# Attention of two blocks: groups in pairs on TensorE, the sink's column as the start of the minimum, scaling on GpSimd

## The reference

```
m = jnp.max(s, axis=-1)
m = jnp.maximum(m, sk)                      # sk: the sink of the head
p = jnp.exp(s - m[..., None])
l = jnp.sum(p, axis=-1) + jnp.exp(sk - m)
p = p / l[..., None]
o = jnp.einsum('bnhgqk,bnkhd->bnqhgd', p, vv)
```

## Time and profile before

| | us |
|---|---|
| median of 3 runs (lowest, highest) | 2098.12 (2096.47, 2103.21) |
| the profiled execution | 2096.36 |
| its span | 2094.6 |
| stage a, scores of group 2 to last sums | 1063.85 to 1127.80 |
| stage b, first scores to last sums | 1610.18 to 1686.30 |

### The profile page before, as it was taken

One profiled execution on the slowest core, in us unless ns is written; L12 is line 12 of the kernel. 1 busy time (PEld: TensorE's weight loads), 2 busy tenths in 40 slices (PEclk: granted clock), 3 DMA queues, 4 the chain that ended last, 5 costly groups with the idle time before them and its releaser, 6 DMA issues.

```text
span 2094.6 us, 28597 instructions
## 1 busy us (share of the span) xinstructions
PE 2059.3 (98%) x10618; PEld 1733.8 (83%) x10618; DVE 986.8 (47%) x1909; ACT 886.8 (42%) x1307; POOL 844.6 (40%) x281
## 2 busy tenths in 40 slices
PE   9999999999999999998999999999999999999998
PEld 6888877888888888884878888888887688888887
DVE  4889688573411111366985344134323934431432
ACT  3355445363443222534366454233423954432332
POOL 3443432444244444442712444444443034444443
PEclk9999999999999999999999999999999999999999
DMA  9654312325233342341202432433422034324322
GB/s 370 243 184 125 101 61 61 94 93 181 72 104 86 104 116 78 111 117 43 79 13 57 120 100 86 115 101 95 145 86 73 2 96 119 101 79 122 100 73 88
DMA packets 303799, 219.63 MB, mean 105 GB/s; under 512 B 13568, under 2 KB 288128, under 8 KB 301408
## 3 DMA queue, kind: packets, MB, share of 16 engines
q1 hardware_dynamic: 293216, 195.67, 31.1%
q10 hardware_dynamic: 10496, 22.81, 3.5%
HBM read 213.48 MB, written 2.10 MB: 103 GB/s over the span
## 4 chain that ended last, share of the span: by engine, by line
PE 64%; issue 18%; DVE 10%; POOL 5%; ACT 3%; ACTq 0%; POOLq 0%; DMA 0%; DVEq 0%
PE bank L900 51%; POOL w_split L2783 5%; PE bank L1123 2%; PE bank L1313 2%; PE bank L1335 2%; DVE bank L2280 2%; DVE arena L2743 1%; DVE small L2741 1%; DVE bank L2243 1%; PE bank L1322 1%; PE bank L1171 1%; DVE bank L2222 1%; POOL w_split_out L2783 1%; PE bank L1418 1%; PE bank L1271 1%
## 5 line engine op out<-in xcount | busy, mean ns | idle before, releaser
L900 PE MATMUL bank<-h_hi,w_split 128*128 128x512 f32 x3696 | 1119.3, 381 | 0.7 <-POOL w_split L2783 0.7
L2783 POOL TENSOR_TENSOR w_split<-wslots,w_split 128x2048 fp32r<-128x2048 f32 (+3 forms) x174 | 712.7, 4096 | 971.1 <-ACT w_split L1581 530.5
L900 PEld LDWEIGHTS bank<-h_hi,w_split 128*128 128x128 f32 x3696 | 698.0, 189 | 116.6 <-issue 17.5
L900 PE MATMUL bank<-h_lo,w_split 128*128 128x512 f32 x1848 | 701.3, 379 | 0.0
L900 PEld LDWEIGHTS bank<-h_lo,w_split 128*128 128x128 f32 x1848 | 349.3, 189 | 52.7 <-issue 5.2
L900 PE MATMUL bank<-hid_hi,w_split 128*128 128x512 f32 x1056 | 315.8, 379 | 1.9 <-DVE hid_lo L2525 1.9
L1602 ACT ACTIVATE w_split<-wslots 128x2048 fp32r<-128x2048 f32 (+2 forms) x80 | 141.3, 1767 | 367.9 <-PE bank L900 367.9
L1581 ACT ACTIVATE w_split<-wslots 128x2048 fp32r<-128x2048 f32 (+3 forms) x91 | 158.7, 1744 | 312.8 <-PE bank L900 287.1
L900 PEld LDWEIGHTS bank<-hid_hi,w_split 128*128 128x128 f32 x1056 | 199.6, 189 | 31.5 <-DVE hid_lo L2525 3.2
L900 PE MATMUL bank<-hid_lo,w_split 128*128 128x512 f32 x528 | 200.1, 379 | 0.0
L2243 DVE SCALAR_TENSOR_TENSOR bank<-arena,cols,bank 128x512 f32<-128x512 f32 x240 | 161.4, 749 | 5.5 <-ACT bank L1695 4.9
(11 more groups left out here) (342 smaller groups left out, 2353.3 us busy)
## 6 DMA issues: line engine op xcount, KB each, us to landing
wslots<-in_f_w_up SPq DMA_DIRECT2D x88, 512.0 KB, 4.8
wslots<-in_w_in SPq DMA_DIRECT2D x24, 1024.0 KB, 5.4
wslots<-in_w_ffn_up SPq DMA_DIRECT2D x44, 512.0 KB, 4.6
arena<-in_w_ada ACTq DMA_DIRECT2D x8, 2048.0 KB, 8.9
wslots<-in_f_w_down SPq DMA_DIRECT2D x16, 768.0 KB, 4.8
wslots<-in_a_w_in SPq DMA_DIRECT2D x10, 1024.0 KB, 5.2
wslots<-in_f_w_down SPq DMA_DIRECT2D x16, 640.0 KB, 4.5
arena<-in_w_ada_first SPq DMA_DIRECT2D x8, 1024.0 KB, 18.9
```

Of the source, the lines that this page charges most:

```text
L900: return nc.tensor.matmul(bank[:], w, woven(x), start=start, stop=stop)
L2783: last = nc.gpsimd.tensor_tensor(part[:, 1, cols_of], slot(p, 1, size)[:, 0, cols_of], part[:, 0, cols_of].bitcast(F32), ALU.subtract)
```

## The change

TensorE takes the groups in pairs: step i is scores(2i), scores(2i+1), turn(2i-3), turn(2i-2), sums(2i-5), sums(2i-4). On DVE the minimum of a group with a sink begins from the sink's column, so `lowest` goes; the reciprocal hands over to GpSimd, which scales the probabilities; the copies of odd groups go to DVE, those of even groups stay on ACT, each with a semaphore of its own. GpSimd's first four pieces of the output weights follow the groups 30 to 33, the second four the last group. The memory queries' pieces move to before the first turns. Two semaphores of memsets become one.

```diff
@@ TensorE, attend
-                for g in range(len(groups) + SUM_LAG):
-                    if g < len(groups):
-                        scores(g)
-                    if g in FILL_AT:
-                        next(fill)
-                    if g in early:
-                        early[g]()
-                    if LAG <= g < len(groups) + LAG:
-                        turn(g - LAG)
-                    if g >= SUM_LAG:
-                        sums(g - SUM_LAG)
+                steps = len(groups) // 2
+                for i in range(steps + 3):
+                    of_groups = lambda part, first: [part(g) for g in (first, first + 1) if 0 <= g < len(groups)]
+                    of_groups(scores, 2 * i)
+                    if i in (steps, steps + 1):
+                        next(fill)
+                    if ("turn", i) in early:
+                        early["turn", i]()
+                    of_groups(turn, 2 * i - 3)
+                    if i in (steps, steps + 1):
+                        next(fill)
+                    if ("sums", i) in early:
+                        early["sums", i]()
+                    of_groups(sums, 2 * i - 5)
...
+            def queries_end():
+                mem_queries(2 * DT - 3)
+                mem_queries(2 * DT - 2)
+
+            attend(2, b_fill, {("turn", 0): queries_end, ("turn", 1): lambda: mem_queries(2 * DT - 1),
+                               ("sums", 2): lambda: wait_emptied(pe, "b_qmem")})
@@ ScalarE, attend
-                    if with_sink:
-                        act.wait_ge(S["at_lowest"], g + 1)
-                    else:
-                        act.wait_ge(S["at_logits"], n + 1)
+                    act.wait_ge(S["at_logits"], n + 1)
...
-                for g in range(len(groups) + SUM_LAG):
+                for g in range(len(groups) + 6):
                     if g < len(groups):
                         exps(g)
-                    if LAG <= g < len(groups) + LAG:
-                        copies(g - LAG)
-                    if g >= SUM_LAG and (g - SUM_LAG) % TB == TB - 1:
-                        outputs(g - SUM_LAG)
-                    if g - len(ATTENTION[k]) in SPLIT_AT:
...
+                    if g % 2 == 0 and 2 <= g < len(groups) + 2:
+                        copies(g - 2)
+                    if g % TB == 0 and g >= 2 * TB:
+                        outputs(g - 5)
+                    if g in SPLIT_AT:
...
@@ VectorE, attend
-                        ins = nc.vector.tensor_tensor_reduce(out=out, in0=src, in1=mask, scale=-grp["scale"], scalar=-NEG, op0=op, op1=ALU.min,
+                        least = -NEG if sink is None else cols[:, COL["sinks"] + sink + e:COL["sinks"] + sink + e + 1]
+                        ins = nc.vector.tensor_tensor_reduce(out=out, in0=src, in1=mask, scale=-grp["scale"], scalar=least, op0=op, op1=ALU.min,
...
-                    steps.did(nc.vector.reciprocal(stat(n, 0, ne), stat(n, 4, ne)))
+                    nc.vector.reciprocal(stat(n, 0, ne), stat(n, 4, ne)).then_inc(S["at_inverse"], 1)
...
+                def copies(g):
...
+                    dve.wait_ge(S["at_turned"], n + 1)
+                    if n >= 3:
+                        dve.wait_ge(S["at_sums"], n - 2)
+                    w = groups[g]["n"]
+                    nc.vector.tensor_copy(probs_turned[:, n % 3, 0:w], banks[6 + n % 2][:, 0:w]).then_inc(S["odd_copied"], 1)
...
+                for g in range(len(groups) + 8):
                     if g < len(groups):
                         logits(g)
                     if 1 <= g <= len(groups):
                         inverses(g - 1)
...
+                    if g == 3 and early:
                         early()
...
+                    if g % 2 and 5 <= g < len(groups) + 4:
+                        copies(g - 4)
+                    if g % TB == 2 and g >= 10:
+                        lower(g - 7)
@@ GpSimd
+            def attend(k, output):
+
+                g0, groups = GROUPS_BEFORE[k], ATTENTION[k] + ATTENTION[k + 1]
+                for g, grp in enumerate(groups):
+                    n = g0 + g
+                    pool.wait_ge(S["at_inverse"], n + 1)
+                    for e, (lo, w) in enumerate(grp["heads"]):
+                        part = probs[:, n % RING, lo:lo + w]
+                        last = nc.gpsimd.tensor_scalar(part, part, stat(n, e), None, ALU.mult)
+                    last.then_inc(S["at_probs"], 1)
+                    if 30 <= g < 34:
+                        lower_piece(output, ahead(output), g - 30)
+                for piece in range(4):
+                    lower_piece(output, 1 - ahead(output), piece)
```

More of the change, by code:

```diff
@@ L2011, in copies @@
                     w = groups[g]["n"]
[L2012 removed]
+                    nc.scalar.activation(probs_turned[:, n % 3, 0:w], banks[6 + n % 2][:, 0:w], ACT.Copy).then_inc(S["even_copied"], 1)
                 def outputs(g):
@@ L2627, in inverses @@
                     dve.wait_ge(S["at_exp"], n + 1)
-                    steps.did(nc.vector.reciprocal(stat(n, 0, ne), stat(n, 4, ne)))
-                def weights(g):
+                    nc.vector.reciprocal(stat(n, 0, ne), stat(n, 4, ne)).then_inc(S["at_inverse"], 1)
+                def copies(g):
                     n = g0 + g
-                    steps.settle()
-                    for e, (lo, w) in enumerate(groups[g]["heads"]):
-                        part = probs[:, n % RING, lo:lo + w]
-                        last = nc.vector.tensor_scalar(part, part, stat(n, e), None, ALU.mult)
-                    last.then_inc(S["at_probs"], 1)
+                    dve.wait_ge(S["at_turned"], n + 1)
[3 more added lines that the diff above has]
+                    nc.vector.tensor_copy(probs_turned[:, n % 3, 0:w], banks[6 + n % 2][:, 0:w]).then_inc(S["odd_copied"], 1)
                 def lower(g):
@@ L2643, in lower @@
                     nc.vector.tensor_tensor(out, unit_bank(n // TB)[:], upper.bitcast(F32), ALU.subtract).then_inc(S["at_low"], 1)
-                for g in range(len(groups) + SUM_LAG + 1):
+                for g in range(len(groups) + 8):
                     if g < len(groups):
@@ L2650, in attend @@
                         inverses(g - 1)
-                    if g < len(groups):
-                        lowest(g)
-                    if 1 <= g <= len(groups):
-                        weights(g - 1)
-                    if g == LAG and early:
+                    if g == 3 and early:
                         early()
-                    if g > SUM_LAG and (g - SUM_LAG) % TB == 0:
-                        lower(g - SUM_LAG - 1)
+                    if g % 2 and 5 <= g < len(groups) + 4:
+                        copies(g - 4)
+                    if g % TB == 2 and g >= 10:
+                        lower(g - 7)
             def ffn(k):
```

55 lines of the change are left out of this document (26 added, 29 removed).

## The result

The changed kernel takes 2117.82 us, median of 4 runs (2115.89 to 2119.52), beside 2099.55 for the kernel before (2096.47 to 2103.21): ratio 1.0077 [1.0064, 1.0090]. It is slower by 0.8%, where 2088 us (2080 to 2098) was forecast. The profiled execution has a span of 2114.3 us against 2094.6.

What follows compares the result with a forecast made beforehand. TensorE, 98% busy, was taken as the bound, with DVE and ACT close. Window gains 1.5 + 0.4 + 1.7 + 2.3 + 0.9 + 2.6 = 9.4 us from 2096.36 gave 2087.0, set to 2088 with half the median's surplus; range 2080 to 2098.

Steps and rivals of the forecast that it cites:

- The step that failed: GpSimd's scaling of 256 columns in both attention stages: 0.40 us, 0.80 a group, with 0.70 as the other end.
- The forecast's loop: Steady stage b: in-order queues tie ACT, DVE and TensorE in a loop over four groups, 6.28 us, above the 5.58 floor.
- the port: Steady stage b: DVE's sink copy waits while GpSimd scales, some 0.2 us, making the loop 6.5 a turn.
- Rival B: Both stages: GpSimd scales at 0.70 us and the loop goes through it, 7.0 a turn; 2094 to 2096 us; chance 0.19.
- Rival D: Both stages, worst in b: scaling over 0.83 us makes GpSimd the bound; about 2112 us at 1.05; chance 0.10.
- Rival C: Both stages: the loop has slack and TensorE runs at its floors; 2081 us; chance 0.14.
- Rival E: TensorE: gaps come with handing over, not tile shape, so pairs keep them; only starts and tails gain, 2093 us; chance 0.05.
- A head: Steady stage a: a head falls from 5.50 to 5.43 us, gaining 0.4 us in that window.
- The pairs: TensorE: changes of tile shape, 0.53 us a group, are paid once for two groups; four b groups' floor 5.58.
- worth nothing alone: ACT: losing half its copies, 0.24 us a group, gains nothing alone because ACT is not what ends last.
- DVE: Group work on DVE: lowest and scaling leave, 0.60 for a copy and 0.06 per column scalar come; 5.6 us in four groups.
- The four pieces: End of stage a: four GpSimd output-weight pieces between the scalings hold an even group once or twice, costing 1.1 us.

Runs made afterwards that it cites:

- x3_constant: The changed kernel with GpSimd multiplying by a constant instead of the reciprocal's column: 2113.74 us, one run.
- x2_forecast: The changed kernel with GpSimd scaling only as many columns as take the forecast time (48 of 256 in 0.40 us), the rest unscaled: 2093.84 us, ratio 0.9963.
- x3_three_quarters: The changed kernel with GpSimd scaling three quarters of each head's columns (192 of 256), the rest unscaled: 2107.38 us, ratio 1.0021.
- x1_pool_only: The kernel before with one part of the change, GpSimd scaling the probabilities, and its output-weight pieces placed as in the change: 2108.30 us, ratio 1.0032.
- x1_pairs_min: The kernel before with only pairs on TensorE and the minimum begun from the sink's column: 2102.02 us, ratio 1.0002.
- x3_two_tensors: The changed kernel with GpSimd's scaling as a product of two tensors, the factor's column repeated along the row: 2097.15 us, ratio 0.9982.
- x2_act_copies: The changed kernel with all copies on ScalarE: 2115.03 us, ratio 1.0065.
- x5_single_two_tensors: The kernel before, single groups, with only the scaling moved to GpSimd, as a product of two tensors: 2097.09 us, ratio 0.9979.
- x1_dve: The changed kernel with the scaling taken back to VectorE: 2120.57 us, ratio 1.0088.
- x4_all: x3_two_tensors with output and rest one step later, even copies behind the odd exponentials, and GpSimd's first pieces spread: 2096.70 us, ratio 0.9966.

## Why the prediction was wrong

- **The step that failed** is the size of one term: "It has one tensor in and one out, as the cast, so I take 0.40, 0.80 a group, and keep 0.70 as the other end." Measured 0.924 and 1.80 a group, above both ends. The cast was taken for its number of inputs; x3_constant shows that the operation sets the rate, and even the two-tensor product (0.61) is quicker. This term is nearly the whole error: from the 9.4 us of gain forecast to the 15.1 of loss are 24.5 us, and with the length as taken, x2_forecast, 23.2 of them are gone. The Trainium skill, "GPSIMD Engine Reference", Performance versus the Vector engine, gives 769 ns for 512 elements as a best case; this trace has 1564 for 512 columns with this operation, so the measurement decides.
- **The forecast's loop** was right: with the size as taken the turn is 6.33 against 6.28 without the port, and the timeline of x2_forecast follows it step by step. With the long scaling another loop, through GpSimd, is longer.
- **Rival B** had the place right, a loop through the scaling, but once through one group: 5.45 + 1.80 = 7.25, and "6.9 with the port 7.0" for the 0.70 it took. The trace and x3_three_quarters show two groups' scalings in it.
- **Rival D** had the condition right (over 0.83), not the mechanism: GpSimd's own work is 6.58 a turn, and the turn is 7.40. Its 2112 stood for 1.05 us; at the 0.924 measured its own terms give 32 x 0.19 + 16 x 0.03 = 6.6 us, under 2105. That 2118 came near 2112 is luck. Its mechanism is that of x1_pool_only, which lost 6.7.
- **Rival C** did not come: no steady turn under 6.02, TensorE's floor is 5.58. **Rival E** fell with the gaps of the pairs in x2_forecast. A head took 5.49 there, as before; 5.43 was forecast.
- **The pairs** save the gaps of tile shape once for two groups: right, the rows of x2_forecast. So is "worth nothing alone": DVE and ACT bind.
- **DVE**: the column scalar lengthens the reduction from 418 to 476 ns, 0.06 as taken; the copy costs 0.60 (0.67 long), as taken. Its work in four groups was reckoned 5.6; in x2_forecast it is busy 28.22 us in five turns, 5.64.
- **The port**: right in kind. The sink copy beside a running scaling took 0.34 and 0.28 us, 0.234 on average against 0.162 in x1_pairs_min. In kind this agrees with the Trainium skill, "SBUF — State Buffer", Who interferes with whom, on 2-port copies. In x2_forecast, with scalings of 0.41, the mean is 0.176, so next to nothing of the 0.2 a turn came there. Beside the two-tensor scaling of x3_two_tensors one sink copy a turn took 0.57, inside the 0.4 to 0.7 named as the outer end.

```profile
1657.93 0.34 DVE L2610 COPY arena<-cols 128x2 f32<-128x2 f32 x1
...
1658.90 0.28 DVE L2610 COPY arena<-cols 128x2 f32<-128x2 f32 x1
```

The same copy in x3_two_tensors:

```profile
1645.82 0.57 DVE L2610 COPY arena<-cols 128x2 f32<-128x2 f32 x1
```

- **The four pieces** among the scalings were reckoned 1.1 us in stage a. With the long scaling TensorE waited 1.68 and 1.83 us behind them:

```profile
1120.20 0.66 PE L1320 MATMUL bank<-cons,arena 128*128 128x128 f32 x4 [1.68 <-POOL arena L2965]
...
1125.46 0.66 PE L1320 MATMUL bank<-cons,arena 128*128 128x128 f32 x4 [1.83 <-POOL arena L2965]
```

- **The whole** was compared at unlike starts: 4.8 us of the 19.7 us of span lie ahead of stage a. That start varied by 8.6 us among twenty profiles with its code alike, and 4.8 lies within that; no run ties it to the change.

## What to carry to other kernels

An engine's rate for one operation says little about another on it: where the operation itself has no row, neither the number of inputs nor the nearest row gives a bound, and its price should be measured first, and its other forms too. Ask of a slower instruction how often the in-order loop passes through it: the same scaling made four groups 0.06 us longer in the old order and 0.75 in pairs. And an order that frees one engine is worth nothing until the next ones, here DVE at 98% and ACT at 96%, are relieved as well.

## What the runs showed of the hardware

- GpSimd, 128 rows of float32: `tensor_scalar` 0.28 us and 2.5 ns a column with a column as factor (314 ns for 8, 604 for 128, 924 for 256, 1564 for 512), 851 ns for 256 with a constant; `tensor_tensor` with a repeated column 398, 613 and 1040 ns for 128, 256 and 512.
- ACT scales 256 columns in SBUF in 0.40 us from start to start, not far under its exponentials with their sums (0.50).
- The granted clock lay at 0.50 for 3.4 or 6.8 us in the start of stage a in all twenty profiles. In stage b it was full before, and fell in five others: 3.4 us in the start and 3.4 in the end in the changed kernel, 7 and 3.4 in x2_act_copies, 7 in the start of x5_single_two_tensors, 3.4 in the end of x1_dve and of x4_all. The falls in the ends of the changed kernel, x1_dve and x4_all came after TensorE was busy 0.24 to 0.54 of 2 us.
- A DVE copy of two columns took 0.162 us on average where GpSimd does not scale (x1_pairs_min), 0.234 beside `tensor_scalar` of 0.92 us (the changed kernel), and 0.57 once a turn beside `tensor_tensor` of 0.61 us (x3_two_tensors).
